# A Conformer depthwise convolution moved from VectorE and GpSimd to 32-column tiles on TensorE

## What is computed

```python
CONFORMER_CONV_WIDTH = 31
def causal_depthwise_conv(x, w):     # y[t] = sum_k w[k] * x[t-(K-1)+k]
    ...
def layer_norm(x, g, b):
    mu = jnp.mean(xf, axis=-1, keepdims=True)
    xc = xf - mu
    var = jnp.mean(xc * xc, axis=-1, keepdims=True)
    y = xc * lax.rsqrt(var + LN_EPS)
    return (y * g + b).astype(x.dtype)
def conformer_conv_module(h, w_pw1, b_pw1, w_dw, b_dw, ln_g, ln_b, w_pw2, b_pw2):
    a, g = jnp.split(h @ w_pw1 + b_pw1, 2, axis=-1)
    u = a * jax.nn.sigmoid(g)
    u = causal_depthwise_conv(u, w_dw) + b_dw
    u = jax.nn.silu(layer_norm(u, ln_g, ln_b))
    return u @ w_pw2 + b_pw2
```

## Time and profile before

| | us |
|---|---|
| time, median of 3 runs (2618.64 to 2618.74) | 2618.66 |
| span of the profiled execution | 2615.8 |
| PE busy | 2465.8 (94%) |
| DVE busy | 1405.0 (54%) |
| ACT busy | 916.1 (35%) |
| POOL busy | 1076.1 (41%) |
| DVE taps, line 1646, 142 instructions | 167.2 |
| granted TensorE clock, mean | 0.959 |

### The profile page before, as it was taken

The page is one execution under the profiler, slowest core; times in us unless marked ns, Lnnn a source line. Parts: engine busy times, 40 slices in busy tenths (PEclk is TensorE's granted clock), DMA queues, the critical chain, the costliest instruction groups (busy, mean ns, idle before and its releaser), DMA issues.

```text
span 2615.8 us, 30678 instructions
## 1 busy us (share of the span) xinstructions
PE 2465.8 (94%) x10898; PEld 1979.5 (76%) x10898; DVE 1405.0 (54%) x1717; ACT 916.1 (35%) x1377; POOL 1076.1 (41%) x462
## 2 busy tenths in 40 slices
PE   8999899999957589999989999999999999999997
PEld 6777688887745368888868887878888677788886
DVE  4353644411899745442155765577731566577711
ACT  5432422222437442222242244433322455333322
POOL 3223444444479144444444211444444212344443
PEclk9999899999888789999989999999999889999999
DMA  4112233332210023333323211333333211233222
GB/s 144 57 51 79 69 96 97 98 91 89 73 57 1 24 65 96 96 96 96 92 69 93 65 33 33 97 94 97 97 92 95 67 33 54 91 97 97 96 90 80
DMA packets 57824, 204.87 MB, mean 78 GB/s; under 512 B 6544, under 2 KB 7056, under 8 KB 57744
## 3 DMA queue, kind: packets, MB, share of 16 engines
q1 hardware_dynamic: 57456, 203.41, 25.4%
q10 hardware_dynamic: 288, 0.36, 0.0%
HBM read 201.65 MB, written 2.10 MB: 78 GB/s over the span
## 4 chain that ended last, share of the span: by engine, by line
PE 52%; issue 28%; POOL 10%; DVE 9%; ACT 1%; DMA 0%; POOLq 0%; DVEq 0%; SPq 0%
PE bank L442 17%; PE bank L444 16%; PE bank L443 16%; POOL w_lo L367 9%; DVE by L1646 6%; DVE h L1416 1%; PE bank L648 1%; DVE u_lo L1398 0%; PE bank L633 0%; DVE ba L1628 0%; PE bank L641 0%; POOL m L384 0%; PE bank L719 0%; DVE m L1406 0%; DVE by L1643 0%
## 5 line engine op out<-in xcount | busy, mean ns | idle before, releaser
L367 POOL TENSOR_TENSOR w_lo<-raw,w_hi 128x1024 fp32r<-128x1024 f32 x376 | 940.5, 2507 | 1458.2 <-ACT w_hi L947 1458.2
L442 PE MATMUL bank<-u_hi,w_hi 128*128 128x512 f32 x1952 | 782.2, 401 | 38.2 <-POOL w_lo L367 20.9
L443 PE MATMUL bank<-u_lo,w_hi 128*128 128x512 f32 x1952 | 773.6, 396 | 0.0
L444 PE MATMUL bank<-u_hi,w_lo 128*128 128x512 f32 x1952 | 772.5, 396 | 0.0
L947 ACT ACTIVATE w_hi<-raw 128x1024 fp32r<-128x1024 f32 x378 | 395.6, 1056 | 894.8 <-PE bank L444 873.7
L442 PEld LDWEIGHTS bank<-u_hi,w_hi 128*128 128x128 f32 x1952 | 375.9, 193 | 126.5 <-DVE u_lo L1398 23.0
L444 PEld LDWEIGHTS bank<-u_hi,w_lo 128*128 128x128 f32 x1952 | 374.7, 192 | 80.3
L443 PEld LDWEIGHTS bank<-u_lo,w_hi 128*128 128x128 f32 x1952 | 375.7, 192 | 78.7 <-issue 1.2
L444 PE MATMUL bank<-hid_hi,w_lo 128*128 (+1 forms) x704 | 280.9, 399 | 0.0
L443 PE MATMUL bank<-hid_lo,w_hi 128*128 (+1 forms) x704 | 277.4, 394 | 0.0
L442 PE MATMUL bank<-hid_hi,w_hi 128*128 (+1 forms) x704 | 276.0, 392 | 0.0
(11 more groups left out here) (277 smaller groups left out, 2774.7 us busy)
## 6 DMA issues: line engine op xcount, KB each, us to landing
raw<-weights_dram SPq DMA_DIRECT2D x378, 512.0 KB, 3.6
h<-x_t_dram SPq DMA_DIRECT2D x8, 256.0 KB, 6.4
out_dram<-m SPq DMA_DIRECT2D x8, 256.0 KB, 2.2
ap<-select_dram SPq DMA_DIRECT2D x1, 512.0 KB, 9.2
vec<-vectors_dram SPq DMA_DIRECT2D x1, 343.0 KB, 8.4
cmask<-masks_dram ACTq DMA_DIRECT2D x1, 224.0 KB, 2.7
dist<-squares_dram ACTq DMA_DIRECT2D x1, 128.0 KB, 2.2
identity<-squares_dram SPq DMA_DIRECT2D x1, 64.0 KB, 7.7
```

The costliest lines, as they stand in the source:

```text
L367: pool.tensor_tensor(w_lo[:, j, :], raw[:, j, :], w_hi[:, j, :].bitcast(F32), ALU.subtract)\
L442: pe.matmul(out, wh, xh, start=start, stop=False)
L443: pe.matmul(out, wh, xl, start=False, stop=False)
L444: return pe.matmul(out, wl, xh, start=False, stop=stop)
```

## The change

The gated chunk goes to a ring of three (`bz`, `CONV_RING`). For each chunk SP copies it in 16 DMAs into `bz4`: for each of the four groups g of 32 features, four copies on partitions 32i to 32i+31, copy i shifted by i tokens. One matmul over all 128 partitions then does four taps (i = 0 to 3) of one group, with a 128 x 32 block `bw` in which row 32i+f has tap 4q+i of feature f in column f; eight steps q give 31 taps, four groups g fill the 128 output partitions of one bank. The blocks are made by POOL, one product of 128 x 1024 a chunk, from the taps `bwv` (16 small DMAs and four of an identity, once) and `eye`. The matmuls are plain float32. `conformer_order` (in place of `tap_order`) puts the convolution of chunk c-2 behind the slots of chunk c on PE and on DVE. The passes over diagonals, the taps on DVE and POOL, and ACT's part of both are gone.

LayerNorm: DVE takes a shift off each chunk as it leaves the bank (the mean over the first 128 features), and sums chunks and squares as they come, so that PE adds three operands and not sixteen; the variance is the mean square less the squared mean. The subtraction of the mean moves between the multiplications of the output projection's start.

```diff
+SHIFTS = 4
+GROUPS = P // 32
+STEPS = (LONG_TAPS + SHIFTS - 1) // SHIFTS
+REACH = T + SHIFTS * (STEPS - 1)
+CONV_RING = 3
+CONV_LAG = 2
...
+def conformer_order():
+    items = []
+    for c in range(KC):
+        items += [("slot", 2 * c), ("slot", 2 * c + 1), ("gated", c)]
+        if c >= CONV_LAG:
+            items.append(("conv", c - CONV_LAG))
+    return items + [("conv", c) for c in range(KC - CONV_LAG, KC)]
...
+            def shift_gated(c):
+                b = c % CONV_RING
+                sp.wait_ge(bz_ready, c + 1)
+                if c >= CONV_RING:
+                    sp.wait_ge(conv_full, GROUPS * (c - CONV_RING + 1))
+                for g in range(GROUPS):
+                    for i in range(SHIFTS):
+                        sp.dma_start(bz4[32 * i:32 * i + 32, b, g, :], bz[32 * g:32 * g + 32, b, i:i + REACH])\
+                          .then_inc(bz4_landed[b], 16)
...
+            load_taps()
+            for c in range(KC):
+                for s in (first + RING + 2 * c, first + RING + 2 * c + 1):
+                    load_next(s)
+                shift_gated(c)
...
+            def tap_blocks(c):
+                b = c % CONV_RING
+                if c >= CONV_RING:
+                    pool.wait_ge(conv_full, GROUPS * (c - CONV_RING + 1))
+                rows = bwv[:, :, c:c + 1].to_broadcast([P, GROUPS * STEPS, 32])
+                cols = eye[:, :].unsqueeze(1).to_broadcast([P, GROUPS * STEPS, 32])
+                pool.tensor_tensor(bw[:, b, :, :], rows, cols, ALU.mult).then_inc(bw_ready, 1)
...
-                    product(bank[5 + i][:, :], dg_hi[:, n % 4, :], dg_lo[:, n % 4, :], bz_hi[:, i, tap:tap + T],
-                            bz_lo[:, i, tap:tap + T], tap == 0, tap == LONG_TAPS - 1).then_inc(dg_used, 1)
...
+            def depthwise(c):
+                b = c % CONV_RING
+                out = bank[5 + b]
+                pe.wait_ge(bw_ready, c + 1)
+                pe.wait_ge(bz4_landed[b], LANDED * (c // CONV_RING + 1))
+                if c == CONV_RING:
+                    pe.wait_ge(conv_made, 1)
+                elif c > CONV_RING:
+                    pe.wait_ge(xc_ready, c - CONV_RING + 1)
+                for q in range(STEPS):
+                    for g in range(GROUPS):
+                        last = pe.matmul(out[32 * g:32 * g + 32, :], bw[:, b, g * STEPS + q, :],
+                                         bz4[:, b, g, SHIFTS * q:SHIFTS * q + T], start=(q == 0), stop=(q == STEPS - 1))
+                        if q == STEPS - 1:
+                            last.then_inc(conv_full, 1)
...
+            pe.wait_ge(b_sums, KC - 2)
+            pe.matmul(STAT[:, :], ones[:, :], bsum[:, :], start=True, stop=False)
+            pe.wait_ge(b_squares, KC - 2)
+            pe.matmul(bank[7][:, :], ones[:, :], acc[:, :], start=True, stop=False)
+            pe.wait_ge(xc_ready, KC)
+            pe.matmul(STAT[:, :], ones[:, :], by[:, KC - 1, :], start=False, stop=True).then_inc(mean_full, 1)
+            pe.wait_ge(sq_ready, SQ["b_var"] + KC)
+            pe.matmul(bank[7][:, :], ones[:, :], sq[:, (KC - 1) % 2, :], start=False, stop=True).then_inc(var_full, 1)
...
+                dve.wait_ge(conv_full, GROUPS * (c + 1))
+                dve.scalar_tensor_tensor(out=by[:, c, :], in0=bank[5 + c % CONV_RING][:, :], scalar=col("b_dw", c),
+                                         in1=bshift[:, :], op0=ALU.add, op1=ALU.subtract).then_inc(xc_ready, 1)
```

More of the change, by code:

```diff
@@ L345, in _, with loads @@
             sp.dma_start(select_raw, select_d).then_inc(consts_landed, 16)
[L346 to L350, removed]
+            def loads(a, b):
+                with sp.Fori(a // RING, b // RING) as i:
+                    for j in range(RING):
+                        sp.wait_ge(slot_done, RING * (i - 1) + j + 1)
+                        sp.dma_start(raw[:, j, :], weights[bass.ds(RING * i + j, 1)].rearrange("o p n -> p (o n)"))\
+                          .then_inc(raw_landed[j], 16)
@@ new lines, in _ @@
+            loads(RING, first - first % RING)
+            for s in range(first - first % RING, first + RING):
+                load_next(s)
+            load_taps()
+            for c in range(KC):
+                for s in (first + RING + 2 * c, first + RING + 2 * c + 1):
+                    load_next(s)
+                shift_gated(c)
+            last = first + RING + 2 * KC
+            for s in range(last, last + -last % RING):
+                load_next(s)
+            loads(last + -last % RING, N_SLOTS - N_SLOTS % RING)
@@ L705, in _ @@
-            for n, c in enumerate(CONV_ORDER):
-                if c in PE_CHUNKS:
-                    pe.wait_ge(tap_evac, PE_CHUNKS.index(c) + 1)
-                elif c == POOL_CHUNK:
-                    pe.wait_ge(pool_taps, LONG_TAPS - 1)
-                elif c == SHARED:
-                    pe.wait_ge(taps, len(TAP_DONE) + 1)
-                else:
-                    pe.wait_ge(taps, TAP_DONE[c, LONG_TAPS - 1])
-                last = pe.matmul(STAT[:, :], ones[:, :], by[:, c, :], start=(n == 0), stop=(n == KC - 1))
@@ new lines, in _ @@
+            for what, n in B_ITEMS[2:]:
+                if what == "slot":
+                    if n >= 4:
+                        pe.wait_ge(b_evac, n - 3)
+                    chunk(SLOT["b_in"] + n, 0, bank[n % 4][:, :], u_hi, u_lo)
+                    if n == 2:
+                        mean_square("b_pre")
+                    if n == 2 * CONV_LAG + 3:
+                        pe.wait_ge(conv_made, 1)
+                        pe.matmul(STAT[:, :], ones[:, :], by[:, 0, :], start=True, stop=True).then_inc(shift_full, 1)
+                elif what == "conv":
+                    depthwise(n)
@@ L1198, in _ @@
-            act.wait_ge(sq_used, USED["b_var"] + KC)
-            root("b_var", e=1)
+            act.wait_ge(var_ready, 1)
+            root("b_var", src=bvar, scale=1.0, e=1)
+            act.preload_act_table_set("silu_and_others")
             for c in range(KC):
```

287 lines of the change are left out of this document (116 added, 171 removed).

## The result

| | before | changed |
|---|---|---|
| time, median of 4 runs, us | 2618.65 (2616.67 to 2618.74) | 2574.99 (2573.64 to 2577.43) |
| ratio, 95% interval | | 0.9846 (0.9827 to 0.9865) |
| profiled execution: time, span, us | span 2615.8 | 2577.43, 2575.6 |
| PE / DVE / ACT / POOL busy, us | 2465.8 / 1405.0 / 916.1 / 1076.1 | 2465.2 / 1263.3 / 857.5 / 1003.6 |
| last tile pass, in the trace | | 843.38 (forecast 815.7) |

The change makes the kernel 1.5% faster, 43.7 us. The forecast was 2553, 65.8 us less. The convolution on PE does what was forecast of it; 22 of the 65.8 us did not come. The spans differ by 40.2 us and the medians by 43.7: the profiled execution of the change is the slowest of its four, 2.4 us above their median.

A forecast was written before the change was run, and what follows sets the result against it. DVE's taps bound the convolution. On PE, ten slots 54.4, shift 0.9, convolutions 58.9 and waits 5 after 696.5 give 815.7; plus 24.5, 840.2 against 906.0: -65.8 from 2618.66, 2553 us, range 2543 to 2600.

The forecast's parts named there:

- The bound: Conformer layer's convolution, before the change: the stage lasts as long as DVE's taps, 57.2% of the chain, 167.2 us.
- The cost of a chunk: Convolution on PE: 64 passes, four at once, 6.91 us plus 0.45 for narrow tiles; 7.36 a chunk, 58.9 for eight.
- Four at once: Convolution on PE: a step's four column groups overlap fully, extended from two tiles at L891; 16 x 0.432 us a chunk.
- one or two at a time: Convolution overlap rivals: one, 28.1 us a chunk, 2719, chance 0.07; two, 14.3, 2608, chance 0.13 together with a 1.2 GHz clock.
- Weight loads at nothing: Convolution on PE: loads hide inside passes, cost nothing; rival of exposed loads 2.2 us a chunk, 2571, chance 0.08.
- The side chain through SP: Copies, weight load, split, sigmoid, gate: 14.2 us a turn against PE's 18.3, so it does not bound.
- the break at 0.56: SP's copies: the time per issue, in us, above which SP's chain takes over; each 0.1 more costs 13.5 us.
- SP's chain takes over: Rival on SP's queue: 0.75 us an issue adds 26 us, 2579; at 1.0 us 2613; chance 0.12.
- The start: Before the first convolution: ACT waits behind the taps' small transfers, taken as 5 us, bounds 0 and 15.
- The short row: Evidence for the wait at the start: a transfer of 128 small packets landed in 1.8 us; 5 us was taken nearer it.
- The tail: Last pass to output projection: 10.1 us instead of 16.65; first two projection slots 14.4 us; ending 24.5 after the pass.
- Range and sign: Whole kernel: 2543 to 2600 us, chance 0.80; faster 0.87, same 0.05, slower 0.08.

The follow-up runs named there:

- group_by_group: The changed kernel with a chunk's passes reordered, all 16 steps of one group of 32 columns before the next group's: 2670.72 us, ratio 1.0199.
- half_on_act: The changed kernel with the copies of groups 2 and 3 issued by ACT on its own queue, behind each chunk's sigmoid: 2554.15 us, ratio 0.9764.
- two_groups: The changed kernel with the 16 steps of groups 0 and 1 alternating, then those of groups 2 and 3: 2587.64 us, ratio 0.9886.
- sigmoid_first: The changed kernel with ACT making a chunk's sigmoid before it splits the next weight slot: 2551.95 us, ratio 0.9742.
- sigmoid_twenty: sigmoid_first with four more copies a chunk into a tile nobody reads, 20 issues instead of 16: 2556.34 us, ratio 0.9769.

## Why the prediction was right and wrong

**Right.** The bound: DVE's taps went out of the chain. The cost of a chunk: "16 x 0.432 = 6.91 us, and for entering and leaving the narrow tiles 0.45" is 16 x 0.429 and 0.2, 7.07 instead of 7.36. Four at once was the step on which all hung, drawn from two tiles at L891, and both rivals against it (one or two at a time) fell. Put into that order by hand, the kernel is indeed slower than before (2670.7), or loses 13 us (2587.6), but both prices (2719 and 2608) were too high: a chunk takes 22.57 and 12.25 us instead of 28.1 and 14.3, because passes overlap at each change of group.

**Weight loads at nothing** held. A chunk's loads start every 0.43 us and end inside the passes. In group_by_group passes follow each other on the same columns and the same rows every 0.429 us, no further apart than the full-width passes of the earlier trace rows (0.432 for 512 columns), with a load of 0.11 us before each hidden. The Trainium skill, "TensorE: Matmul & The Clock Gate", section "Part 3: Packing small matmuls", has weight loads overlap only where the row groups differ, and the trace disagrees. Nor does its 2.38 times for three column tiles carry over to here: four tiles are 3.9 times one (64 x 0.429 against 7.07).

**The failed step: "The side chain through SP".** The loop was there, link by link, and so was its slope ("each 0.1 us more costs 13.5 us"). Its terms were too small. An issue was taken at 0.474 us from DRAM loads; a copy from SBUF to SBUF takes 0.63. That is above the break at 0.56 that the prediction itself had worked out. Copies and landing together take 14.15 us a turn instead of 11.7. The gate was taken at 0.75 from the earlier trace rows; in that trace it always starts before POOL's instruction or without one. Here it starts behind POOL's split and takes 2.28 to the next copies. So a turn has 18.2 to 18.7 us instead of 14.2. The rival "SP's chain takes over" had the mechanism and a price of 2579 for 0.75 us an issue; it is what happened, at 2575, and had a chance of 0.12. Its price came near by luck: at the 0.63 us that an issue took, its slope gives 9 us and 2562; the gate's 1.5 us a turn, 10.7 in seven turns, and the half clock made up the rest. Opening the loop gives 2551.95, 1 us from the forecast of 2553, which had taken the loop as covered. That is partly luck too: in its trace PE still waits 4.1 us for copies, where the forecast had 5 us for the taps, which did not come.

**The start**: "I take 5" for the taps' small packets was 0.1. ACT waited 1.04 us for raw at 680.98 and then for PE; the transfers of bwv landed in 1.9 us, no slower than the 128-packet row. The short row was the near one, and the 15 us bound was empty.

**The half clock** was not in the sum at all, beyond what the rows of before had in them. Passes at 1.2 GHz came with the three longer waits in this stretch and cost 6.8 us together, and the first projection slots ran at half clock too. A rival of waits should be priced with the slow passes behind them, here three tenths on top of the waits themselves.

**The tail**: 10.3 for 10.1 (the terms given for it add up to 9.9); the two slots 16.4 for 14.4, nine of these microseconds (853.67 to 862.6) at half clock.

**Range and sign** held: 2543 to 2600, faster. That the time also touches the end of the forecast's own range (2543 to 2575) is luck: that end stood for 15 us of waits for the taps and 1.4 us more a chunk, and neither came.

## What to carry to other kernels

When a queue issues many small transfers and its in-order successors feed the engine that produces the next transfers, write the loop down with every link, and price an issue from the same kind of transfer; where no row has one, see what a third more would do. If the loop and the bounding engine have nearly the same period (18.7 and 18.1 here), the loss shows only at the ends, and the cheapest cure is to cut one link: moving a 0.7 us sigmoid ahead of a split was worth 23 us (it opened the loop, and it took the gate out of POOL's way); splitting the copies over two queues, with the gate as slow as ever, was worth 21. Small column tiles want neighbours in program order on different columns; the same passes in another order cost 96 us.

## What the runs showed of the hardware

- **A copy's issue costs the same whatever its size, and not what a load's does.** On SP, start to start: 16 loads of the taps from DRAM, 32 rows each, 0.48 us (four in 1.90); copies of 32 rows from SBUF to SBUF 0.63 us, with 2160 or 32 bytes a row alike. In half_on_act ACT's queue issues them at nearly the same pace (8 in 5.28 us) while SP issues its own 8 in 4.96.
- **At a change of column groups, passes of the next groups run beside the last four steps of the old ones.** By the starts these are four passes at each change in group_by_group (52 steps instead of 64) and eight at the one change in two_groups (28 instead of 32).
- **The gate and POOL.** The gate takes 0.75 us alone and 2.3 behind POOL's split of the same moment: DVE's and POOL's rows,
```profile
707.75 2.30 DVE L1648 SCALAR_TENSOR_TENSOR bz<-ba,vec 128x512 f32<-128x512 f32 x1 [14.99 <-ACT ba L1177]
```
```profile
707.11 2.39 POOL L394 TENSOR_TENSOR w_lo<-raw,w_hi 128x1024 fp32r<-128x1024 f32 x1 [16.10 <-ACT w_hi L970]
```
  The gate ends at 710.05, 0.55 us after POOL's split (709.50), as if it had begun only then. The Trainium skill, "SBUF — State Buffer", section "Terms", says that VectorE and GpSimd share a port pair under an exclusive lock and that the loser fully blocks; the rows agree. The same 0.55 us stands behind POOL's end for every gate of the changed kernel. Who comes first decides: in the kernel before, gates that start 0.2 us ahead of POOL's instruction take 0.74, and in sigmoid_first, ahead of the split, 0.75. What the slow gate costs by itself (1.5 us a turn of the loop) is read from rows: no run took it away and left the loop.
- **Half clock behind a wait.** Where PE had waited 4.64, 5.37 and 10.02 us, the changed kernel's chunk behind the wait took 9.20, 8.37 and 9.41 us instead of 7.07, with the granted clock at half for a part of it; behind 3.34 us it took 7.07. Other kernels agree: 8.54 us behind 5.12 in half_on_act, 9.13 behind 5.08 and 9.77 behind 3.95 in sigmoid_twenty, 7.07 behind 3.08 in sigmoid_first. Nothing was run to test this apart.
